# Six of seven q, k, v projection slabs by Strassen's block products in a hybrid retention and attention block

## What is computed

```python
hn = rms_norm(h, mix_norm_g)
proj = hn @ w_in                     # [1040, 1024] @ [1024, 6656]
rq, rk, rv, rg, sq, sk, sv, gr, gs = jnp.split(proj, split_points, axis=-1)
y_ret = retention(pad(rq), pad(rk), pad(rv))            # chunks of 128, a state per head
y_swa = sliding_window_attention(pad(sq), pad(sk), pad(sv), q_norm_g, k_norm_g, sinks)
```

## Time and profile before

| | |
|---|---|
| three runs, median (lowest to highest) | 1709.89 us (1707.38 to 1711.13) |
| the profiled execution, its own time | 1713.22 us |
| span of that execution, first to last instruction | 1711.5 us |
| TensorE busy | 1667.8 us, 97%, 7968 matmuls |
| VectorE busy | 924.8 us, 54% |
| ScalarE busy | 745.0 us, 44% |
| GpSimd busy | 392.4 us, 23% |
| mean granted clock of TensorE | 0.994 of full speed |
| DMA | 204 MB, 119 GB/s over the span |

### The profile page before, as it was taken

How to read it: one execution, slowest core, us unless ns; L and a number is a source line. 1 busy time by engine, 2 the same in 40 slices (tenths; PEclk the granted TensorE clock), 3 DMA queues, 4 the chain that set the end, 5 groups by cost and what they waited for, 6 DMA issues and landing times.

```text
span 1711.5 us, 22479 instructions
## 1 busy us (share of the span) xinstructions
PE 1667.8 (97%) x7968; PEld 1382.1 (81%) x7968; DVE 924.8 (54%) x1708; ACT 745.0 (44%) x1528; POOL 392.4 (23%) x591
## 2 busy tenths in 40 slices
PE   7999999999999999999999999999999999999999
PEld 6777888888878888787788888778888888888887
DVE  4311256522355666655555435966666655766775
ACT  5322245523356666656112214655455554444442
POOL 1000000110027777676321000212121223200000
PEclk9999999999999999999999999999999999999999
DMA  6111112121123433334655323144443459843463
GB/s 196 50 49 49 40 65 101 67 85 50 49 65 62 107 73 93 89 71 109 200 168 179 105 62 111 74 154 163 157 154 135 142 204 367 297 115 95 127 192 99
DMA packets 110101, 204.08 MB, mean 119 GB/s; under 512 B 12576, under 2 KB 46416, under 8 KB 110000
## 3 DMA queue, kind: packets, MB, share of 16 engines
q1 hardware_dynamic: 72688, 104.88, 20.1%
q0 software_dynamic: 37312, 97.89, 18.1%
HBM read 139.55 MB, written 54.53 MB: 113 GB/s over the span
## 4 chain that ended last, share of the span: by engine, by line
PE 88%; DVE 6%; DMA 3%; ACT 1%; issue 1%; POOL 0%; SPq 0%; DVEq 0%; ACTq 0%
PE bank L752 26%; PE bank L757 26%; PE bank L756 26%; PE bank L967 2%; DMA RAW<-in_w_in 2%; PE bank L1003 1%; DVE WL L1639 1%; PE bank L981 1%; PE bank L1011 1%; DVE WL L2113 1%; DMA TH<-gates 0%; PE bank L783 0%; PE bank L788 0%; PE bank L996 0%; PE bank L880 0%
## 5 line engine op out<-in xcount | busy, mean ns | idle before, releaser
L1639 DVE TENSOR_TENSOR WL<-RAW,WH 128x512 fp32r<-128x512 f32 x152 | 99.7, 688 | 150.4 <-ACT WH L1191 149.5
L752 PE MATMUL bank<-WH,HN 128*128 128x512 f32 x448 | 176.9, 395 | 3.7 <-DVE HN L1664 2.3
L757 PE MATMUL bank<-WL,HN 128*128 128x512 f32 x448 | 175.2, 391 | 0.0
L756 PE MATMUL bank<-WH,HN 128*128 128x512 f32 x448 | 175.2, 391 | 0.0
L752 PE MATMUL bank<-WH,ADH 128*128 128x512 f32 x448 | 174.3, 389 | 0.0
L756 PE MATMUL bank<-WH,ADL 128*128 128x512 f32 x448 | 174.3, 389 | 0.0
L757 PE MATMUL bank<-WL,ADH 128*128 128x512 f32 x448 | 174.3, 389 | 0.0
L636 POOL TENSOR_SCALAR PR<-PR,RC 128x272 f32<-128x272 f32 x128 | 125.1, 1009 | 175.8 <-DVE RC L1953 175.4
L752 PE MATMUL bank<-HN,WH 128*128 128x512 f32 x384 | 153.2, 399 | 1.3 <-DVE WL L1639 1.3
L756 PE MATMUL bank<-HN,WL 128*128 128x512 f32 x384 | 151.0, 393 | 0.0
L757 PE MATMUL bank<-HN,WH 128*128 128x512 f32 x384 | 150.9, 393 | 0.0
(11 more groups left out here) (302 smaller groups left out, 3816.3 us busy)
## 6 DMA issues: line engine op xcount, KB each, us to landing
ARAW<-uop SPq DMA_DIRECT2D x112, 256.0 KB, 3.3
RAW<-in_w_in SPq DMA_DIRECT2D x104, 256.0 KB, 3.1
uop<-US POOLq DMA_DIRECT2D x64, 256.0 KB, 2.7
WRAW<-in_w_up SPq DMA_DIRECT2D x15, 1024.0 KB, 5.7
gates<-TB POOLq DMA_DIRECT2D x48, 256.0 KB, 2.4
uop<-UA POOLq DMA_DIRECT2D x48, 256.0 KB, 2.7
TH<-gates POOLq DMA_DIRECT2D x32, 256.0 KB, 3.0
RAWD<-in_w_down SPq DMA_DIRECT2D x32, 256.0 KB, 4.5
```

The costliest lines, as they stand in the source:

```text
L752: mm = pe.matmul(bank, ahi, bhi, start=first, stop=False, skip_group_check=onto)
L756: pe.matmul(bank, alo, bhi, start=False, stop=False, skip_group_check=onto)
L757: return pe.matmul(bank, ahi, blo, start=False, stop=last, skip_group_check=onto)
L1639: dve.tensor_tensor(WL[:, k, :], RAW[:, k % 4, :], WH[:, k, :].bitcast(F32), ALU.subtract)\
```

## The change

The slabs 1 to 3 and 6 to 8 are computed in three pairs: retention k with attention k/v, both halves of retention v, both halves of attention q. A pair is [1024 x 1024] by [1024 x 1024], cut into halves each way and computed by seven products of 512x512 blocks instead of eight (`st_product`). A product is 4 token blocks by 4 inner tiles by three matmuls, with 4 weight tiles. The sums of rows of `HN` (`half_sum`) are made once, by VectorE, from float32 copies that ScalarE takes beside the casts of slab 0; each is split again into `SHI` and `SLO`. The sums of weight tiles (`add_y`, `st_sum`, `add_raw`) are made for each pair; VectorE and ScalarE combine the products' banks into the four result blocks (`evict`, `result`, `kept_diff`). All seven result slabs go to a DRAM tensor `proj` and come back: the retention's share before and during retention, attention's share during retention (q) and after it (k, v). The small matmuls for meta rows are made in four of the seven products (32 rows by 8 matmuls each) for two pairs, and also go through DRAM. The squares for the q and k norms are taken during the products.

Stage 4 above is gone. What it covered is done while 36 of the 256 gate steps run ahead of attention; 220 remain for its 67 steps. The last chunk of retention no longer updates the state. The loops over slabs and chunks are written out.

TensorE's products and the banks they wait for:

```diff
-            with pe.Fori(1, 4) as c:
-                for b in range(NB):
-                    dense_a("M", 8 * c + b, B[b % 2], 0, hn_block(b), c, b == 0, b == NB - 1)
+            for g in range(NSG):
+                for t in range(7):
+                    st_product(g, t)
...
+            def st_bank(g, t, f):
+                if t % 2 == 0:
...
+                    return B[f]
+                i = 12 * g + 4 * (t // 2) + f
+                if i >= 2:
+                    g2, u, f2 = (i - 2) // 12, (i - 2) // 4 % 3, (i - 2) % 4
+                    if u == 1:
+                        pe.wait_ge(ps_act, 16 * g2 + 8 + f2 + 1)
+                    else:
+                        pe.wait_ge(ps_dve, 12 * g2 + 4 * u + f2 + 1)
+                return B[4 + i % 2]
+            def st_product(g, t):
+                if g == 0 and t in QUAD:
+                    pe.wait_ge(hs_lo, t - 1)
+                for f in range(4):
+                    bank = st_bank(g, t, f)
+                    for k in range(4):
+                        if f == 0:
+                            pe.wait_ge(w_ready, st_n(g, t, k) + 1)
+                        mm = three(bank[:, :], hi, lo, WH[:, w, :], WL[:, w, :], ...)
+                if meta:
+                    meta_rows(g, t)
```

ScalarE during and after slab 0, with a second eviction of each transposed half:

```diff
+                    if b < NB:
+                        hi = act.copy(SR[:, 2 * (b // 4) + u, :, ...], B[2 + u][:, :]...)
+                    hi.then_inc(hn_hi, 1)
+            for i, q in enumerate((0, 3, 2, 1)):
+                act.wait_ge(hs_sum, 3 if i == 0 else 4)
+                act.copy(SHI[:, q, :, :], SR[:, q, :, :]).then_inc(hs_hi, 1)
```

VectorE, with two half sums ahead of the meta rows' low part and two behind the first weights:

```diff
+                    half_sum(0, 3, 2, 3, ALU.subtract)
+                    half_sum(1, 2, 0, 2, ALU.subtract)
                 lo_x(b + 1)
+            for k in range(4):
+                st_lo(0, 0, k)
+            half_sum(2, 0, 3, 0, ALU.subtract)
+            half_sum(3, 1, 1, 0, ALU.add)
+            for g in range(NSG):
+                for k in range(4):
+                    st_lo(g, 1, k)
+                if g == 0:
+                    half_lo(0)
+                for k in range(4):
+                    add_y(g, k)
+                st_sum(g, 2, 0)
+                st_sum(g, 2, 1)
+                st_lo(g, 2, 0)
+                result(g, 1, 0)
```

SyncE's loads for the first pair, right behind those of slab 0:

```diff
+                    sp.dma_start(PX[:, :, :], quarter(c0, 0)).then_inc(px_full, 16)
+                for k in range(4):
+                    sp.dma_start(RAW[:, k, :], ...)
+                    sp.dma_start(PY[:, :, :], quarter(c1, 0)).then_inc(py_full, 16)
+                sp.dma_start(PZ[:, :, :], quarter(c1, 1)).then_inc(pz_full, 16)
```

VectorE behind the last product:

```diff
+                    for f in range(4):
+                        reduce_sq(g, 6, f)
+            dve.wait_ge(mu_full, MU0 + 32)
             dve.tensor_tensor(MRK[0:META, :, :], MRK[0:META, :, :], MU[0:META, :, :], ALU.add)
```

GpSimd's queue at the end of retention:

```diff
+            pool.wait_ge(o_full, NB + START)
+            load_kv(0)
+            load_kv(1)
+            pool.dma_start(MKV[0:META, :], mrow[3, 0:META]).then_inc(mu_full, 16)
+            pool.dma_start(MU2[0:META, :], mrow[3, META:2 * META]).then_inc(mu_full, 16)
+            pool.wait_ge(oraw_rdy, NB + START)
+            pool.dma_start(y_raw[NB - 1], RT[:, 2:4, NB - 1, :]).then_inc(yraw_done, 16)
```

TensorE, then ScalarE, between retention and attention:

```diff
-            for b in range(NB):
-                dense_a("M", ACT_C + b, B[b % 2], 0, hn_block(b), SLAB_C, b == 0, b == NB - 1)
+            ahead = {18: transpose_meta_k, 25: transpose_new_k, 28: transpose_q}
+            for i in range(BR):
+                gate_step(i)
+                if i in ahead:
+                    ahead[i]()
+            act.wait_ge(meta_sum, 4)
+            act.activation(ST[0:META, 0:256], MKV[0:META, 0:256], ACT.Square).then_inc(c_sq, 1)
+            act.wait_ge(yraw_done, 16 * NB)
+            act.copy(MVT[0:META, :, 0, :], MKV[0:META, 256:512]...).then_inc(c_sq, 1)
+            act.wait_ge(scr_step, 2)
+            act.activation(SCR[:, :, :], SCR[:, :, :], ACT.Sqrt, bias=EPSC[:, 0:1]).then_inc(c_std, 1)
+            root(25, SSM[0:META, 0:4])
+            gate_ahead(0)
+            act.wait_ge(qf_rdy, 1)
+            hi_k(META).then_inc(qh_rdy, 1)
+            hi_q(0)
+            hi_kn(0)
+            gate_ahead(1)
```

More of the change, by code:

```diff
@@ L424, in _, with load_slab @@
         def _(sp):
[L425 removed]
+            def load_slab(slab, source):
                 for k in range(KT):
[L428 to L430 removed]
+                    if k >= 4 or slab > 1:
+                        sp.wait_ge(w_ready, wn(slab, k) - 3)
                     sp.dma_start(RAW[:, k % 4, :], source(k)).then_inc(raw_full[k % 4], 16)
@@ new lines, in _ @@
+            pool.wait_ge(w_ready, 8 + W0)
+            pool.wait_ge(mu_full, MU0)
+            for rows, tile in ((0, MRK), (META, MU)):
+                pool.dma_start(tile[0:META, :, :], mrow[0:3, rows:rows + META].rearrange("s p c -> p s c"))\
+                    .then_inc(mu_full, 16)
+            pool.wait_ge(ps_full, 28 * NSG - 4)
+            for par in range(2):
+                pool.wait_ge(gst_done[par], 16 * GS0)
+            pool.wait_ge(pst_a, 16 * 12 * (NSG - 1))
+            pool.wait_ge(pst_b, 16 * 4 * (NSG - 1))
@@ L850, in _ @@
             mm.then_inc(u_full, 1)
-            with pe.Fori(0, 2) as it:
+            pe.wait_ge(ps_act, PA0)
+            for it in range(2):
                 for r in range(4):
@@ new lines, in _, with evict @@
+                act.copy(TB[:, b % 2, :], B[b % 2][:, :]).then_inc(a_free, 1)
+            for i, q in enumerate((0, 3, 2, 1)):
+                act.wait_ge(hs_sum, 3 if i == 0 else 4)
+                act.copy(SHI[:, q, :, :], SR[:, q, :, :]).then_inc(hs_hi, 1)
+            def evict(g, t, f):
+                act.wait_ge(ps_full, 28 * g + 4 * t + f + 1)
+                dest = SB[f] if t == 2 else SA[f]
+                if t == 2:
+                    act.wait_ge(pst_b, 16 * 4 * g)
+                elif t == 0 and g == 0:
+                    for par in range(2):
+                        act.wait_ge(gst_done[par], 16 * GS0)
+                else:
+                    act.wait_ge(pst_a, 16 * (12 * g + {0: 0, 3: 4, 6: 8}[t]))
+                bank = B[f] if t % 2 == 0 else B[4 + (12 * g + 4 * (t // 2) + f) % 2]
+                if t == 6 and g == 2:
+                    squares(g, t, f, bank)
+                act.copy(dest[:, :], bank[:, :]).then_inc(ps_act, 1)
@@ new lines, in result @@
+            def result(g, t, f):
+                dve.wait_ge(ps_full, 28 * g + 4 * t + f + 1)
+                if t == 1:
+                    dve.wait_ge(ps_act, 16 * g + f + 1)
+                elif t == 4:
+                    dve.wait_ge(ps_d, 4 * g + f + 1)
+                bank = B[f] if t == 4 else B[4 + (12 * g + 4 * (t // 2) + f) % 2]
+                tile = st_tile(t, f)
+                if t == 4:
+                    op = dve.tensor_tensor(tile[:, :], tile[:, :], bank[:, :], ALU.subtract)
+                else:
+                    op = dve.tensor_tensor(tile[:, :], bank[:, :], tile[:, :], ALU.add)
+                op.then_inc(ps_dve, 1)
@@ L1704, in _ @@
             dve.tensor_copy(STA[:, SL:2 * SL], B[7][:, :]).then_inc(st_rdy, 1)
-            with dve.Fori(0, 2) as it:
+            for it in range(2):
                 for r in range(4):
```

806 lines of the change are left out of this document (544 added, 262 removed).

## The result

| | before | after |
|---|---|---|
| median (lowest to highest), same chip | 1710.12 us (1707.38 to 1711.13, 4 runs) | 1688.07 us (1686.93 to 1688.95, 4 runs) |
| ratio, 95% interval | | 0.987 (0.986 to 0.989) |
| the profiled execution, its own time | 1713.22 us | 1688.95 us |
| span of that execution | 1711.5 us | 1687.2 us |

A forecast was written before the change was run, and what follows sets the result against it. The prediction took TensorE's matmuls to set nearly every stretch. Its terms, -34.0 + 8.3 + 6.0 - 1.4 + 5 = -16.1 us, gave 1694 us, with its own range 1685 to 1703 and 1682 to 1708 for 8 in 10.

The forecast's parts named there:

- The matmuls: Whole kernel: 144 fewer matmuls from three pairs (32.6 us) and no last state update (1.4 us), together -34.0 us.
- rival 3: Product stretches: VectorE and ScalarE handing over weight tiles set the time, TensorE waits in each product; 1728 us, chance 10%.
- The first pair: Slab 0 and first pair: start, weights, result 0, x loads and clock price add +8.3 us in all.
- The wait for result 0: Third block of product 1, first pair: TensorE waits while result 0 queues behind other VectorE work, +4.0 us.
- The -0.8 at the start: Start of product 0: half sums 1.2 us late, against slab 1's 2.02 us ScalarE weight wait disappearing; net -0.8 us.
- The x loads: Slab 0: x blocks land later beside 3 MB of pair loads on SyncE's queue; +2 us, bounds 0 and +6.
- Products to retention: Gap before retention: TensorE idle 3.8 us for the meta sum and scaled keys, plus 2.2 for the clock; +6.0 us.
- The clock's price: After the gap before retention: matmuls run at the lower clock, costing +2.2 us beyond the wait itself.
- Retention: Retention stretch: its inputs through DRAM are issued well ahead, so their loads cost 0 us.
- Preparation: Attention prepared behind 36 gate steps: a new wait replaces today's idle time; net -1.4 us, bounds -4 and +5.
- The wait at gate step 16: Gate steps ahead of attention: TensorE waits 2.0 us for a bank, plus half a clock price, 3.1 in all.
- Attention: Attention with 108 fewer matmuls: less time per step and at slab changes adds +5 us, bounds 0 and +15.

The follow-up runs named there:

- the shifted kernel: Kernel before with one function changed: its 256 gate steps spread over attention up to 11 steps ahead of the even spread; 1699.8 us, ratio 0.995.
- the 16 further ones: Changed kernel with 52 instead of 36 gate steps run ahead of attention; 1691.9 us, ratio 0.991 to the kernel before.

## Why the prediction was right, and where it wasn't

**The matmuls (-34.0)** were right: the count is exact, and pairs 2 and 3 take what their matmuls take, with no wait. That VectorE is busy 60% of the products' window (149.3 of 249.4 us) and never late in these pairs bears out the walk through its list against rival 3.

**The first pair (+8.3, measured +6.7).** The wait for result 0 was named with its place and cause; it is 3.33 us for 4.0, with 7 slow matmuls behind it (1.4 us for 2.2). The wait on product 1's weights (0.9) did not show. The -0.8 at the start was misread: it credits the change with ScalarE's wait of 2.02 us in slab 1, but what TensorE loses there is 0.78 us (at 70.58), so this term should have been +0.4. The x loads were mis-sized: about +0.5 for +2.0. The rows had not separated the cases. The Trainium skill ("DMA: Bandwidth & Descriptors", Queues, rings and completion order) says that each DMA engine takes turns between queues, and by that the term was near 0. The term came out near that end; but the x loads did land later (12.4 us at worst against 7.6 with the pair's loads held back), and no run here shows the turns themselves.

**Products to retention (+6.0, measured +8.0).** The wait is 3.77 for 3.8. The clock's price behind it was mis-sized: 2.2 was taken from ten slow matmuls; here the clock fell ahead of eight meta matmuls, which took 3.78 instead of 1.99 us, and of twelve more (12 x 0.2 = 2.4): about 4.2.

**Retention (0, measured +4.0)** is the step that failed. "I take 0 for these" looked at whether the loads through DRAM land in time for their own readers, and they do. It did not ask which other transfers they make late: the weight blocks of the next slab, then ScalarE's queue, then TensorE, at 400.68, with 8 slow matmuls behind.

**Preparation (-1.4, measured -3.8).** The wait at gate step 16 is 0.76 us and not 2.0, with no clock price: the store and ScalarE's chain behind it end 1.2 us earlier than worked out. The sign and the place were right.

**Attention (+5, measured -1.6)** has the largest error, and two things hide in it. Behind its first scores its waits over 0.15 us add up to 9.8 us before, with 10 slow matmuls at the third slab change, and to 8.0 with none after. The prediction took the slab changes to get worse with fewer gate steps. Instead the changed spread of gate steps moved them, and the kernel before loses 7.6 us of its median by where its own stand. Against the shifted kernel the change's attention costs 7.6 - 1.6 = 6 us beside its matmuls, near the forecast term. That is 0.17 us for each of the 36 steps, where the 16 further ones cost 0.4 each. By the traces alone it is 10 us: from the first transposes of q to the first branch matmul the shifted kernel takes 305.6 us where before takes 317.3, 11.7 less, but the trace of before is that of an execution 3.1 us above its median. Either is a difference between kernels, worked out and not measured in one. If the changed kernel owes to its own spread what the shift gave the kernel before, about a third of the 22 us is not the seven products' but the spread's that came with them. No run of the changed kernel with another spread tests that; shown is that 1699.8 us was to be had with one function changed.

**Behind attention (0, measured -3.6)**: before has waits of 1.77 and 4.03 us with 8 and 13 slow matmuls behind them, after 0.99, 0.97 and 3.35 with 8. The instructions are the same, and from the first branch matmul to the end the traces of the changed kernels take 904.9 to 909.3 us, those of the kernel before and its variants 907.2 to 910.3. I put the difference down to the waits and the clock of single executions; no run separates them.

The errors by parts are -1.6, +2.0, +4.0, -2.4, -6.6 and -3.6 us and add up to -8.2 in the traces, where before was 3.1 us above its median and after 0.9. The forecast of the median was 6 us high, inside its own range (1685 to 1703). That it came so close is in part luck: errors of +6.0 us (the clock at the gap, the late weight blocks) stand against -14.2 us of the other way, of which 10.2 are in attention and behind it, with causes that are open in part.

## What to carry to other kernels

A wait at a stage's border costs twice when matmuls follow it at the lower clock: look first for what the waited-for engine does ahead of the needed result, and move that, as two edits of a few lines gave 8.0 and 5.9 us here. If a new transfer is hidden from its own reader, ask which older transfers share its time, and whose queue stands behind those. When a change shifts a periodic schedule against another, give the old kernel the same shift before crediting the change with the gain.

## What the runs showed of the hardware

- Behind the idle 3.8 us of the gap the granted clock was 0.50 for 9 us, and slow matmuls follow it in six traces of six; sixteen unread matmuls in the gap kept it at 1.00 and made the whole kernel 5.8 us faster.
- What one wait costs through the clock varies between executions. Behind the wait of 3.3 us in product 1 stand 6 to 8 slow matmuls in six traces and none in one, whose instructions are the same up to there. Behind a wait of 2.5 to 3.4 us ahead of the first gate product stand 6 to 8 in six traces, 14 in two and none in one.
- Loads of 1.5 MB issued by GpSimd at 388.3 and 389.0 us delayed 256 KB weight loads from SyncE's queue (5.8 to 8.5 us to landing for 3.3 to 3.9) enough that ScalarE waited 1.07 and 0.81 us; issued some 8 us later, not at all.
